# Streaming x's high and low parts as one 512-wide operand in the first feed-forward projections and the gates

## What is computed (the reference, cut to what matters)

```python
def swiglu(x, w_gate, w_up, w_down):            # first block; w_gate, w_up: 1024 x 2816
    return (jax.nn.silu(x @ w_gate) * (x @ w_up)) @ w_down
...
    proj = h @ w_in[layer]                       # second block, h = rms_norm(x, mix_norm_g)
    z_a, q, k, v, gate_logits = jnp.split(proj, splits, axis=-1)
...
    y_b = dilated_mixture_attention(q, k, v)
    gates = jax.nn.sigmoid(gate_logits.reshape(b, s, N_BRANCHES, D_MODEL))
    merged = gates[:, :, 0] * (y_a @ w_branch_a[layer]) + gates[:, :, 1] * (y_b @ w_branch_b[layer])
```

## Time and profile before

| | before |
|---|---|
| median of 3 runs | 696.93 us |
| profiled execution, device time | 697.08 us |
| its span | 695.3 us |
| TensorE busy (matmul) | 688.9 us, 99% |
| weight loads busy | 648.5 us, 93% |
| VectorE busy | 461.7 us, 66% |
| ScalarE busy | 374.4 us, 54% |
| DMA queue of the weights | 120.55 MB, 48.3% of 16 engines |

### The profile page before, as it was taken

One profiled execution on the slowest core, in us unless ns is written; L12 is line 12 of the kernel. 1 busy time (PEld: TensorE's weight loads), 2 busy tenths in 40 slices (PEclk: granted clock), 3 DMA queues, 4 the chain that ended last, 5 costly groups with the idle time before them and its releaser, 6 DMA issues.

```text
span 695.3 us, 12189 instructions
## 1 busy us (share of the span) xinstructions
PE 688.9 (99%) x5136; PEld 648.5 (93%) x5136; DVE 461.7 (66%) x738; ACT 374.4 (54%) x567; POOL 35.6 (5%) x33
## 2 busy tenths in 40 slices
PE   9999999999999999999999999999999999999996
PEld 8889999999999998889988898999999999998885
DVE  5975676976666664665674568558598888887422
ACT  6865764755444443456365475445467565555322
POOL 0410121200000000011000000000020000000000
PEclk9999999999999999999999999999999999999999
DMA  8953335355555556446365343434636554556501
GB/s 308 360 213 122 122 105 198 123 192 196 195 196 192 184 196 227 181 160 227 138 234 171 141 129 119 178 129 175 242 137 252 188 182 182 184 184 240 181 1 60
DMA packets 19958, 124.17 MB, mean 179 GB/s; under 512 B 2240, under 2 KB 3520, under 8 KB 5696
## 3 DMA queue, kind: packets, MB, share of 16 engines
q1 hardware_dynamic: 18000, 120.55, 48.3%
q10 hardware_dynamic: 1904, 2.85, 1.3%
HBM read 122.34 MB, written 1.05 MB: 177 GB/s over the span
## 4 chain that ended last, share of the span: by engine, by line
PE 98%; issue 1%; ACT 0%; POOL 0%; POOLq 0%; DVE 0%; ACTq 0%
PE pm L317 52%; PE psc L317 33%; PE ptr L317 8%; PE po L317 3%; PE ptr L320 1%; PE po L320 0%; PE psc L320 0%; PE pm L1662 0%; PE psc L1662 0%; ACT yo L323 0%; ACT sq L326 0%; POOLq L175 0%; POOL rcol L329 0%; POOL ones L355 0%; DVE rms L332 0%
## 5 line engine op out<-in xcount | busy, mean ns | idle before, releaser
L329 DVE TENSOR_TENSOR wl<-raw,wh 128x1024 fp32r<-128x1024 f32 (+1 forms) x226 | 270.3, 1209 | 44.2 <-ACT wh L326 34.5
L326 ACT ACTIVATE wh<-raw 128x1024 fp32r<-128x1024 f32 (+1 forms) x226 | 228.9, 1036 | 55.4 <-PE psc L317 34.5
L317 PE MATMUL pm<-xh,wh 128*128 128x256 f32 x560 | 158.4, 283 | 0.0
L317 PE MATMUL pm<-xl,wh 128*128 128x256 f32 x560 | 156.4, 279 | 0.0
L317 PE MATMUL pm<-xh,wl 128*128 128x256 f32 x560 | 156.3, 279 | 0.0
L317 PEld LDWEIGHTS pm<-xh,wh 128*128 128x128 f32 x560 | 105.3, 188 | 2.8 <-issue 2.5
L317 PEld LDWEIGHTS pm<-xl,wh 128*128 128x128 f32 x560 | 105.3, 188 | 0.0
L317 PEld LDWEIGHTS pm<-xh,wl 128*128 128x128 f32 x560 | 105.3, 188 | 0.0
L317 PE MATMUL psc<-xh,wh 128*128 128x256 f32 x304 | 84.9, 279 | 0.0
L317 PE MATMUL psc<-xl,wh 128*128 128x256 f32 x304 | 84.9, 279 | 0.0
L317 PE MATMUL psc<-xh,wl 128*128 128x256 f32 x304 | 84.8, 279 | 0.0
(11 more groups left out here) (300 smaller groups left out, 1230.5 us busy)
## 6 DMA issues: line engine op xcount, KB each, us to landing
raw<-in_w_dram SPq DMA_DIRECT2D x109, 1024.0 KB, 4.8
early<-in_w_dram SPq DMA_DIRECT2D x2, 1024.0 KB, 12.8
raw<-in_w_dram SPq DMA_DIRECT2D x3, 512.0 KB, 7.6
bias<-in_rel_dram ACTq DMA_DIRECT2D x1, 1024.0 KB, 7.9
xa<-in_xt_dram SPq DMA_DIRECT2D x3, 256.0 KB, 6.6
out_dram<-yo SPq DMA_DIRECT2D x3, 256.0 KB, 2.3
raw<-in_w_dram SPq DMA_DIRECT2D x2, 256.0 KB, 4.0
fgb<-in_fin_dram ACTq DMA_DIRECT2D x1, 512.0 KB, 3.9
```

Source lines behind the costliest of these rows:

```text
L317: return lambda e: e.matmul(dst, lhs, rhs, start=start, stop=stop, skip_group_check=True)
L326: return lambda e: e.activation(dst, src, kind, **kw)
L329: return lambda e: e.tensor_tensor(dst, a, b, op)
```

## The change

x's two parts become one tensor `xq`, [128, 8, 2, 256], high and low part of a channel tile side by side; `xh` and `xl` are views of it. A new function `wide_fm` computes a tile in the form that D1 has: per k one matmul of wh against 512 columns of `xq` into the whole bank, one of wl against 256 columns into its first half. F1 and GT use it. The first half of a bank then holds wh xh + wl xh, the second wh xl. A pair of F1 takes two neighbouring banks, and three such pairs rotate (banks 3 and 4, 1 and 2, 5 and 6 of eight); the order of the first four chunks in halves is kept. After a pair ScalarE copies the second halves of both banks into `tg`, VectorE adds the first halves, which frees the banks, and a third operation multiplies by `rbc`. In GT each of 16 tiles has a bank of M by turns and its own `gate(i)` in every slot: ScalarE copy, VectorE add (frees the bank), VectorE multiply, ScalarE tanh, each on 256 columns. The chunks of F1 and GT join those written 32 bytes further in. D1 gets the banks M[1], M[0], M[2], T. The PSUM tensors become one, so that two neighbouring banks can be read by one instruction.

```diff
-TOKEN_MAJOR = [s for a, b in ((KB, QA), (VA, VA + 4), (Q2, Q2 + 4), (K2, K2 + 4), (V2, V2 + 4)) for s in range(a, b)]
+FURTHER_IN = [s for a, b in ((KB, QA), (VA, VA + 4), (Q2, Q2 + 4), (K2, K2 + 4), (V2, V2 + 4),
+                                 (F1, D1), (GT, BR)) for s in range(a, b)]
...
-        xh = keep("xh", [P, KT, SEQ], f32r)
-        xl = keep("xl", [P, KT, SEQ], f32r)
+        xq = keep("xq", [P, KT, 2, SEQ], f32r)
+        xh, xl = xq[:, :, 0, :], xq[:, :, 1, :]
...
-        M = [Bank(pm[:, i, :]) for i in range(3)]
-        S = [Bank(psc[:, i, :]) for i in range(3)]
-        T, O = Bank(ptr[:, :]), Bank(po[:, :])
+        pall = ctx.enter_context(nc.psum_tensor("pall", [P, 8, 512], fp32))
+        banks8 = [Bank(pall[:, i, :]) for i in range(8)]
+        M, S, T, O = banks8[0:3], banks8[3:6], banks8[6], banks8[7]
...
-            a += SHIFT // 8 if c in TOKEN_MAJOR else 0
+            a += SHIFT // 8 if c in FURTHER_IN else 0
...
+        def wide_fm(s, c0, ks, bank, begin, end, last):
+
+            t = None
+            for i, k in enumerate(ks):
+                hw, lw = piece(wh_ring, s, c0 + k * P, P), piece(wl_ring, s, c0 + k * P, P)
+                after = [lo_chunk[s], tok["xl", k]] + (bank.claim() if begin and i == 0 else [])
+                pe.quiet(mm(bank.ap, hw, xq[:, k, :, :], begin and i == 0, False), *after)
+                final = i == len(ks) - 1
+                f = mm(bank.ap[:, 0:SEQ], lw, xh[:, k, :], False, end and final)
+                if final and (end or last):
+                    t = pe.do(f)
+                else:
+                    pe.quiet(f)
+            if last:
+                pe_chunk[s] = t
+            return t
...
         def feed1(slot):
-            banks = feed_banks([S[0], S[1], T, M[0], M[1], M[2], S[2]])
-            stage_first(slot, banks[:2], "gu")
-            stage_pairs(slot, banks, "gu")
+            first = [3, 1, 5]
+
+            def two(n):
+                b = first[n % 3]
+                return banks8[b:b + 2]
+
+            def part(n, ks, begin):
+                for h in range(2):
+                    tok["gu", n] = wide_fm(slot + 2 * n + h, 0, ks, two(n)[h], begin, not begin, not begin)
+
+            def chunk(i):
+                n, h = divmod(i, 2)
+                tok["gu", n] = wide_fm(slot + i, 0, range(KT), two(n)[h], True, True, True)
+            for i in range(4):
+                when(slot + i, 50, lambda i=i: part(i % 2, range(4 * (i // 2), 4 * (i // 2) + 4), i < 2))
+            for i in range(4, 2 * FT):
+                when(slot + i, 50, lambda i=i: chunk(i))
 
             def scale(n):
-                b = n % 3
+                b, b0 = n % 3, first[n % 3]
                 t3 = tg[:, b, 2:].rearrange("p (a n) -> p a n", a=2)
-                t = tok["fs", n] = dve.do(tt(t3, pairs(banks[n].ap), over2(rbc[:, :]), ALU.mult),
-                                          tok["gu", n], tok["rbc"], *ring_readers[b])
-                banks[n].release(t)
+                t = act.do(func(t3, pall[:, b0:b0 + 2, SEQ:], ACT.Copy), tok["gu", n], *ring_readers[b])
+                t = dve.do(tt(t3, t3, pall[:, b0:b0 + 2, 0:SEQ], ALU.add), t)
+                for bank in two(n):
+                    bank.release(t)
+                tok["fs", n] = dve.do(tt(t3, t3, over2(rbc[:, :]), ALU.mult), t, tok["rbc"])
...
-        stage_down(D1, [S[1], S[2], T, S[0]], "d1")
-        residual(D1, down_ends(D1), [S[1], S[2], T, S[0]], "d1", "mixg", D1 - 1)
+        stage_down(D1, [M[1], M[0], M[2], T], "d1")
+        residual(D1, down_ends(D1), [M[1], M[0], M[2], T], "d1", "mixg", D1 - 1)
...
-        stage_fm(GT, 8, M, "gt")
+        for i in range(2 * KT):
+            when(GT + i, 50, lambda i=i: tok.update(
+                {("gt", i): wide_fm(GT + i, 0, range(KT), M[i % 3], True, True, True)}))
...
-        def gate(n):
-
-            bank = M[n % 3]
-            t = dve.do(tt(gates[:, n, :, :], pairs(bank.ap), over2(rbc[:, :]), ALU.mult),
-                       tok["gt", n], tok["rbc"])
+        def gate(i):
+
+            n, h = divmod(i, 2)
+            bank, g = M[i % 3], gates[:, n, h, :]
+            t = act.do(func(g, bank.ap[:, SEQ:], ACT.Copy), tok["gt", i])
+            t = dve.do(tt(g, g, bank.ap[:, 0:SEQ], ALU.add), t)
             bank.release(t)
-            tok["gate", n] = act.do(func(gates[:, n, :, :], gates[:, n, :, :], ACT.Tanh, scale=0.5), t)
-
-        for n in range(KT):
-            when(GT + 2 * n + 2, 10, lambda n=n: gate(n))
+            t = dve.do(tt(g, g, rbc[:, :], ALU.mult), t, tok["rbc"])
+            tok["gate", n] = act.do(func(g, g, ACT.Tanh, scale=0.5), t)
+
+        for i in range(2 * KT):
+            when(GT + i + 1, 10, lambda i=i: gate(i))
```

More of the change, by code:

```diff
@@ L287, in build @@
         assert e7 <= e4
-        pm = ctx.enter_context(nc.psum_tensor("pm", [P, 3, 512], fp32))
-        psc = ctx.enter_context(nc.psum_tensor("psc", [P, 3, 512], fp32))
-        ptr = ctx.enter_context(nc.psum_tensor("ptr", [P, 512], fp32))
-        po = ctx.enter_context(nc.psum_tensor("po", [P, 512], fp32))
-        M = [Bank(pm[:, i, :]) for i in range(3)]
-        S = [Bank(psc[:, i, :]) for i in range(3)]
-        T, O = Bank(ptr[:, :]), Bank(po[:, :])
+        pall = ctx.enter_context(nc.psum_tensor("pall", [P, 8, 512], fp32))
+        banks8 = [Bank(pall[:, i, :]) for i in range(8)]
+        M, S, T, O = banks8[0:3], banks8[3:6], banks8[6], banks8[7]
         pe, act, dve, pool, spq = (Lane(sem(n)) for n in ("pe", "act", "dve", "pool", "spq"))
```

## The result

| | before | after |
|---|---|---|
| median of 8 runs | 696.78 us (696.41 to 697.02) | 698.61 us (698.06 to 700.87) |
| ratio, 95% interval | | 1.0029 [1.0020, 1.0038] |
| profiled execution, span | 697.08, 695.3 us | 698.32, 696.4 us |

The change makes the kernel 0.3% slower, about 1.8 us. The forecast was 696.6 us and no change that can be told; the range held the time. The executions of the changed kernel are not one cluster: six lie at 698.06 to 698.75 us and two at 700.15 and 700.87; the experiments show what the two groups stand for.

The account below looks back on a forecast made before the run. TensorE, busy 99% of the span, was taken as the bound, so only its matmul rate and new waits count. Blocks -1.6 and GT wait +1.3 gave -0.3 us: 696.6 us for the median, range 694.5 to 699.0.

Parts of the forecast that it names:

- Blocks: F1 and GT: 480 blocks pass at D1's 0.3467 us instead of 0.3500, 1.6 us less.
- the change doesn't do what it says: Rival: F1's and GT's blocks stay at 0.350 us, giving +1.3 and 698.2 us; chance 0.12.
- F1 evacuation: F1: added ScalarE copy and VectorE operation per pair hide under TensorE's 5.55 us; VectorE 81% busy; cost 0.
- The slower rival through F1's round: F1: a pair's round exceeds 5.55 us and TensorE waits; at 5.75, +4.1 in all, 701.0 us; chance 0.12.
- Other banks for D1, interleaved x: D1's new banks, interleaved x and the new PSUM tensor: no instruction comes or goes, cost 0.
- Gates: GT: ScalarE and VectorE lag, so TensorE waits 1.3 us before the second scores of attention pair 1.
- Sum: Whole kernel: -1.6 from blocks plus 1.3 from the gates' wait, -0.3 us; 696.6 for the median; chance 0.46.

Follow-up runs that it names:

- e5: e4 with F1's and GT's chunks no longer written 32 bytes further in, so x lies 32 bytes past its weights; 695.92 us, ratio 0.9986.
- e10: Changed kernel without the 32-byte offset for F1's and GT's chunks, tanh where the change has it; 697.25 us, ratio 1.0004.
- e12: e5 with D1's weight chunks 32 bytes further in, so hq lies 32 bytes short of them; 697.10 us, ratio 1.0001.
- e16: e5 with D1's streamed operand hq moved 32 bytes past its weights; 695.97 us, ratio 0.9985.
- e9: The changed kernel run again, unchanged in what it does; 700.42 us, ratio 1.0051.
- e2: Changed kernel with F1 as before the change (narrow blocks, no added offset), GT and D1's new banks as changed; 698.33 us, ratio 1.0018.
- e4: Changed kernel with each gate's tanh queued one slot later on ScalarE; 697.43 us, ratio 1.0002.
- e1: Changed kernel with GT as before the change, F1 and D1 as changed; 697.51 us, ratio 1.0005.
- e14: e13 with the chunks of F1 and GT alone written 32 bytes further in; 703.16 us, ratio 1.0085.
- e7: e4 with F1's and GT's blocks taken two at a time, two 512-wide matmuls then two 256-wide; 696.21 us, ratio 0.9989.
- e8: Kernel before the change with one 128x1 matmul ahead of D1's first block; 698.09 us, ratio 1.0016.
- e13: e4 with x moved by 224 bytes to remainder 0 and no chunk of any stage written further in; 703.65 us, ratio 1.0092.

## Why the prediction was right or wrong

1. *Blocks* (forecast -1.6): nearly right in size where F1 had the good rate, wrong in its premise. In the profiled execution F1 gained 1.09 us of 1.17; GT gained 0.14 of 0.43, its runs of 16 blocks passing at 0.352 to 0.360. The price 0.3467 was taken "because it is the same pair of matmuls on data laid out in the same way", with the equal remainder of weights and x as a reason for it. The form has two prices, 0.3467 and 0.3533, and the second is above the narrow block's 0.3500: there F1 loses 1.0 us against the narrow form (125.32 against 124.28). An equal remainder is just the layout in which either came up; x 32 bytes past the weights, as it lay before the change added F1 and GT to the offset list, gave 0.3467 in all four profiles that had it (e5, e10, e12, e16). That the profiled execution had the good one was luck: the second profile of the same kernel (e9) had the other. The rival "the change doesn't do what it says" named "a small clash of loads and stream" that could eat the 8 cycles; it came nearest, but looked for it in F1 and GT and not in D1.
2. *F1 evacuation* (0): right. F1 has no gap, VectorE stood at 82% for 81% predicted; the new operations took 0.596, 0.688 us for 0.60 and 0.69. The slower rival through F1's round did not come. (D1's first matmul stood at 247.62, not at 247.8, so the cover at its end was 1.4 us and not 1.6; no wait came of it.)
3. *Other banks for D1, interleaved x* (0): **the step that failed.** "No instruction comes or goes" was taken to mean that D1 keeps its rate, cost 0. D1 took 62.19 us for 61.03: +1.16, 0.3533 us a block for 0.3467. The banks are innocent (e2: 61.03 us in the new ones). D1 was at distance 0 before as well, and fast in the one profile of the kernel before; in the changed kernel it was slow in both profiles and, by the sum, in all thirteen executions. What turned it was F1 on the longer offset list: with F1 off the list (e10), or narrow and off it (e2), D1 is at 0.3467 again and the clusters are those of a fast D1. So the fault is the same as in step 1, a rate held for a property of the form. How the stage before reaches into D1's rate is open.
4. *Gates* (+1.3): right, to 0.1 us. The scores were predicted to start at 422.23 and started at 422.17; copies 3 and 4 at 416.19 and 418.80, measured 416.19 and 418.78. e4 shows the mechanism, a tanh ahead of the next copy in an in-order queue.
5. *Sum*: -0.3 predicted, +1.1 in the span. D1 accounts for 1.16 of the 1.4 us, the smaller gain in GT for 0.3. The median of the eight executions stands 0.3 us above the one that was profiled.

What stays open: what picks the rate in an execution when both are possible (e1 took either, half and half), how a stage's pattern reaches the next, why D1 is slow in e14, why one order of blocks (e7) has its own rate, and the longer executions of e8 and of the kernel before, which were not profiled. Whether 32 bytes is special, or any distance forward would do, was not tried.

The Trainium skill (TensorE: Matmul & The Clock Gate, Step-by-step: what each phase is for) says that TensorE reads weights and the streamed operand through two independent ports, so that a weight load takes nothing from a running matmul. It can't be read as a licence to lay out the two operands at will: moving one of them by 32 bytes changed the block by 0.0067 us, 2%, with the same instructions (e4 and e5). Whether the two ports have a part in it, or where else the two meet, no run shows.

**A better version.** e5 and e16 keep the wide form, drop the offset for F1 and GT and queue the tanh later: 695.92 and 695.97 us, ratios 0.9986 [.9977, .9995] and 0.9985 [.9976, .9994], about 1.0 us below the kernel before and 2.7 below the changed one. Both have BR and W2 in their slowest pattern, 0.5 us in all over the kernel before. That is under the 0.2% that was called the limit of one comparison; two comparisons that agree, and intervals that end below 1, speak for a real gain.

## What to carry to other kernels

When TensorE is busy all the time, the rate of a matmul is not one number per shape: read the steps between starts in each stage, and compare the place of the streamed operand with that of the weights before giving a price from another stage. A stage that the change does not touch can change its rate with what runs before it, so the sum needs a line for it, and one profile of a kernel whose executions cluster is one draw. Where an evacuation goes back and forth between two engines, queue its last step behind the next tile's first one.

## What was not expected of the hardware

- A 512-wide and a 256-wide matmul with their weight loads pass in 0.3467 or in 0.3533 us at the same granted clock of 1.00, with the streamed operand 32 bytes past the weights always in the first (F1 in four profiles, D1 in two), 32 bytes short of them always in the second (F1 in two, D1 in two), and at the same remainder in either. The two slow cases are different patterns, a period of three blocks at the same remainder and of two at 32 bytes short.
- The rate of an untouched stage hangs on what ran before it: D1 0.3533 or 0.3467 us a block with F1's offset or without (changed kernel, e10); BR and W2 22.53, 22.79 or 23.04 us each with GT at -32, 0 or +32.
- The narrow form has it too: 0.1167 us in F2 with x where it lay, 0.1200 with x at distance 0, 3.3 us over the stage (e13, e14); and in BR and W2 0.1173 to 0.1200 with nothing moved.
- The same program has executions 3.3 us apart (e1: 695.9 and 699.2), the size of F1 and D1 both at the slow rate.
